# A two-block language model on one core: the second block's input projection is woven with its convolution and its sparse attention, padded columns are left out, and 11 of 31 convolution taps go to VectorE

## The reference, cut to what matters

```python
proj = rmsnorm_2(h, mix_norm_g) @ w_in                  # 256 x 1024 @ 1024 x 2328
conv_a, conv_b, q, k_c, v_c, k_s, v_s, k_w, v_w, gate_logits = split(proj)   # 512, 512, 512, 6 x 128, 24
# conformer_conv
u = conv_a * sigmoid(conv_b)
y = causal depthwise convolution of u, 31 taps, 512 channels, + b_dw
y_conv = silu(layernorm(y))
# nsa_mixer: 8 heads of 64, 2 key groups
kc, vc = compress_tokens(k_c), compress_tokens(v_c)     # 15 blocks; a 2048 x 128 product, gelu, 128 x 64
o_cmp = softmax(q kc) vc        # q without rotation
o_slc = softmax(q_r k_s) v_s    # rotated; at 256 tokens every block is selected
o_win = softmax(q_r k_w) v_w    # rotated
y_nsa = g0 * o_cmp + g1 * o_slc + g2 * o_win            # g = sigmoid(gate_logits)
h = h + concat(y_conv, y_nsa) @ w_out
```

## Time and profile before

| | us |
|---|---|
| median of 3 runs | 1765.82 |
| lowest and highest of them | 1763.61 and 4126.84 |
| the profiled execution | 1765.62 |
| its span, first to last instruction | 1763.8 |
| PE busy | 1663.6 (94% of the span) |
| DVE, ACT, POOL busy | 1191.0, 876.0, 288.1 |
| mean granted clock of TensorE, as a share of 2.4 GHz | 0.971 |

### The profile page before, as it was taken

How to read it: one execution, slowest core, us unless ns; L and a number is a source line. 1 busy time by engine, 2 the same in 40 slices (tenths; PEclk the granted TensorE clock), 3 DMA queues, 4 the chain that set the end, 5 groups by cost and what they waited for, 6 DMA issues and landing times.

```text
span 1763.8 us, 32178 instructions
## 1 busy us (share of the span) xinstructions
PE 1663.6 (94%) x10882; PEld 1510.2 (86%) x10882; DVE 1191.0 (68%) x2262; ACT 876.0 (50%) x1596; POOL 288.1 (16%) x205
## 2 busy tenths in 40 slices
PE   8799998999999989899899989999999999999997
PEld 7788886999887878788799989998888899999996
DVE  3777556688755452445557947887999877777776
ACT  4743343666556551445455465554444445445444
POOL 3233220011100013100003864552000000000000
PEclk9889989999999998999999999999999999999999
DMA  7332233555563630005254654445777756555654
GB/s 266 109 99 81 73 93 122 161 169 182 181 196 121 211 96 0 1 27 191 73 179 150 206 166 139 146 136 175 244 239 240 222 187 190 185 186 188 187 183 153
DMA packets 88138, 271.38 MB, mean 154 GB/s; under 512 B 9856, under 2 KB 26624, under 8 KB 87680
## 3 DMA queue, kind: packets, MB, share of 16 engines
q1 hardware_dynamic: 65088, 237.01, 42.3%
q10 hardware_dynamic: 22976, 33.36, 5.8%
HBM read 258.80 MB, written 11.53 MB: 153 GB/s over the span
## 4 chain that ended last, share of the span: by engine, by line
PE 79%; DVE 11%; ACT 5%; issue 3%; DMA 1%; ACTq 1%; POOL 0%; DVEq 0%
PE ps_chunk L468 43%; PE ps_misc L468 19%; PE ps_misc L279 6%; PE ps_chunk L279 6%; PE ps_misc L2095 3%; DVE ffn_arena L1326 1%; ACT w_hi L403 1%; DVE w_lo L410 1%; DVE x_lo L666 1%; PE ps_misc L651 1%; DVE mixers_arena L1900 1%; DVE mixers_arena L1901 1%; DVE mixers_arena L1897 1%; DVE mixers_arena L1896 1%; DVE mixers_arena L1899 0%
## 5 line engine op out<-in xcount | busy, mean ns | idle before, releaser
L403 ACT ACTIVATE w_hi<-raw 128x512 fp32r<-128x512 f32 x900 | 554.4, 630 | 530.1 <-PE ps_chunk L468 329.4
L410 DVE TENSOR_TENSOR w_lo<-raw,w_hi 128x512 fp32r<-128x512 f32 x725 | 518.1, 729 | 312.1 <-ACT w_hi L403 302.7
L468 PE MATMUL ps_chunk<-x_hi,w_hi 128*128 128x256 f32 x1856 | 543.6, 293 | 20.2 <-POOL w_lo L410 10.0
L468 PE MATMUL ps_chunk<-x_hi,w_lo 128*128 128x256 f32 x1856 | 530.9, 286 | 0.0
L468 PE MATMUL ps_chunk<-x_lo,w_hi 128*128 128x256 f32 x1856 | 530.5, 286 | 0.0
L468 PEld LDWEIGHTS ps_chunk<-x_hi,w_hi 128*128 128x128 f32 x1856 | 360.9, 194 | 32.5 <-POOL w_lo L410 15.0
L468 PEld LDWEIGHTS ps_chunk<-x_hi,w_lo 128*128 128x128 f32 x1856 | 361.7, 195 | 2.7 <-issue 0.2
L468 PEld LDWEIGHTS ps_chunk<-x_lo,w_hi 128*128 128x128 f32 x1856 | 361.2, 195 | 0.0
L410 POOL TENSOR_TENSOR w_lo<-raw,w_hi 128x512 fp32r<-128x512 f32 x175 | 228.7, 1323 | 498.5 <-ACT w_hi L403 279.1
L468 PE MATMUL ps_misc<-w_hi,hid_hi 128*128 128x512 f32 x520 | 204.3, 393 | 4.8 <-DVE w_lo L410 4.8
L468 PE MATMUL ps_misc<-w_hi,hid_lo 128*128 128x512 f32 x520 | 203.8, 392 | 0.0
(11 more groups left out here) (338 smaller groups left out, 1792.1 us busy)
## 6 DMA issues: line engine op xcount, KB each, us to landing
raw<-in_stream SPq DMA_DIRECT2D x452, 512.0 KB, 3.6
early_rows<-row ACTq DMA_DIRECT2D x64, 128.0 KB, 2.4
row<-early_rows ACTq DMA_DIRECT2D x64, 128.0 KB, 3.7
memory_kv<-mixers_arena ACTq DMA_DIRECT2D x4, 512.0 KB, 2.9
mixers_arena<-in_cmp_w ACTq DMA_DIRECT2D x1, 2048.0 KB, 7.3
mixers_arena<-memory_kv ACTq DMA_DIRECT2D x4, 512.0 KB, 6.9
mixers_arena<-in_consts ACTq DMA_DIRECT2D x1, 1665.0 KB, 6.9
row<-in_rows ACTq DMA_DIRECT2D x3, 512.0 KB, 5.3
```

What stands on the lines that cost most here:

```text
L403: e.activation(w_hi[q % 2][:, s], raw[q][:, s], ACT.Copy).then_inc(made, 1)
L410: e.tensor_tensor(w_lo[q % 2][:, s], raw[q][:, s], w_hi[q % 2][:, s].bitcast(F32), ALU.subtract).then_inc(made, 1)
L468: last = e.matmul(o, stationary[a], moving[b], start=start and i == 0, stop=stop and i == 2, skip_group_check=True)
```

## The change

1. `MIXERS_2_ORDER`, a string of letters, weaves five generators: d (the five chunks of `w_in_2`, now by `dense`), k (keys, compression, tile 0 of the attention), q (tables, queries, tile 1), c (taps by PE, layer norm) and t (taps by VectorE). `multiply` and the 30 fillers go. Half of the `w_lo` work of these chunks goes from DVE to POOL.
2. The order of the chunks is k_c v_c k_s v_s; k_w v_w gates; q; conv_a; conv_b. Two PSUM pairs are used in turn (`pairs=2`).
3. `widths`: the chunk with the gates is split, multiplied and copied out with 280 columns in place of 512, and the first block's last token chunk with 256.
4. Taps 0 to 19 stay on PE, in diagonals of 10 (POOL, 128 x 1280). Taps 20 to 30 are 4 x 11 instructions of DVE which accumulate in PSUM; the bias and PE's sum are added by DVE as well.
5. The loads of tables and positions are issued ahead of those for compression and have a semaphore of their own.

```diff
+CONV_PE = 20
+MIXERS_2_ORDER = ("ddctkdqdqdkdddddqddddddddkddkdkdkdkkkqdcddddkkdkddkddddkdkddddkddddkddddkddqdqddddddddqdddddddqddqdd"
+                  "ddddddqdddddcqtqccttqttcctqkctqtcqckckctkcktqtqtcttctttqtkqqtkttccckcccccccqcqtckctkcqckccqkqqkckcqc"
+                  "kqckcccqkqcqkccckcqcccckcqkqkccckkqq")
...
+        widths = {STREAM["w_in token"][0] + 2: RK_H * RK_N, STREAM["w_in_2 token"][0] + 1: 280}
...
-            first, _ = multiply("w_in_2 feature", False, t)
-            multiply("w_in_2 token", True)
-            split_chunks(first, 5, act_hooks=(copy_hook(first, chunk_rows(Z2)),))
...
-            keep_warm(30)
-            interleave(conv=(0, 2, conv, 2),
...
+            dense_again(first, STREAM["w_out_2"][0])
+
+            def dense_chunks():
+                yield from dense(*STREAM["w_in_2 token"], True, lambda n: Z2[:, n - first, :], by_k=t, pairs=2)
+                yield from dense(*STREAM["w_in_2 feature"], False, lambda n: Z2[:, n - first, :], pairs=2)
+
+            keys, queries, NS = nsa(Z2, first, causal, seen, seen_add, inv, pos_raw, cmpw1, cmpw2, have_2, have_cmp)
+            conv, taps = conv_module(Z2, first)
+            weave(MIXERS_2_ORDER, dense=(0, 4, dense_chunks()), conv=(2, 2, conv), keys=(4, 2, keys()),
+                  queries=(6, 2, queries()), taps=(0, 2, taps))
...
+            def taps_by_dve():
+                while not made:
+                    yield "early"
+                for j in range(CONV_PE, CONV_K):
+                    for k in range(CONV_T):
+                        tap, src = taps[:, k, j:j + 1], U[:, k, j:j + T]
+                        if j == CONV_PE:
+                            sums = dve.do(lambda e, k=k, tap=tap, src=src: e.tensor_scalar(
+                                sums_at[:, k, :], src, tap, None, ALU.mult), made[0], own=False)
+                        else:
+                            to = Y if j == CONV_K - 1 else sums_at
+                            sums = dve.do(lambda e, k=k, tap=tap, src=src, to=to: e.scalar_tensor_tensor(
+                                out=to[:, k, :], in0=src, scalar=tap, in1=sums_at[:, k, :], op0=ALU.mult,
+                                op1=ALU.add), before[k], own=False)
```

442 lines of the change are left out of this document (249 added, 193 removed).

## The result

The changed kernel takes 1736.93 us (median of four runs, 1736.40 to 1746.03) against 1767.35 for the kernel before on the same chip. The ratio of the two is 0.9847, with a 95% interval of 0.9803 to 0.9891; it compares the means of the runs and leaves out one run of the kernel before that took 4126.84 us, so it is not the quotient of the two medians. The forecast was 1728.6 with a range of 1713 to 1746. The profiled execution took 1736.4 us, span 1734.6.

A forecast was written before the change was run, and what follows sets the result against it. PE's queue was taken to bound the kernel (79% of the chain of waits). The second mixer's stage going from 206.0 to 172.5 (-33.5) and -3.5 in the first block gave -37.0 from 1765.62: 1728.6 us, range 1713 to 1746.

The forecast's parts named there:

- rival A: Second mixer's stage: PE's queue holds, locks don't bite; first-half gaps shrink to 7, middle to 58; 1714 us, chance 0.22.
- First block: Last token chunk of the first projection, 256 columns instead of 512: -3.5 us, bounds 0 and 5.3.
- Taps: Second mixer: 44 fewer taps on PE at 0.43 us each, -19.0 us; DVE's taps at 0.445 each.
- Padding: Second projection's 280-column chunk: 48 matmuls at 0.13 instead of 0.23 us, -4.8 us of PE.
- Start of the stage: PE's gaps at unit 2: 3.5 us for ACT's late split and POOL's half, 1.2 for DVE's half behind the tables.
- Diagonals at the keys: First half: POOL's two diagonals stop two-input DVE instructions; PE waits 5 us at the keys' transposes, bounds 0 and 9.
- Half clock of the front: Projection with early steps: PE at half clock costs 1.7 us after the first gap, 3.4 at the compression.
- Middle: Taps and attention after U: both queues walked in order, 64.5 us plus 1.7 for half clock, 66.2 us.
- End: From the layer norm's first transposes to `w_out_2`: PE's queue unchanged, 25.3 us against 25.5 before.
- Rival B: Second mixer: `w_lo` halves and six diagonals on POOL stop DVE, delaying softmaxes; +15 us, 1744 us, chance 0.22.
- Rival C: Second mixer: the weave starves PE, progress under 0.70 makes the stage slower than before; 1777 us, chance 0.04.
- Rival D: DVE's taps make PE wait, first block's saved columns bring 0; +8, 1737 us, chance within the forecast's and B's.

The follow-up runs named there:

- The run with another order: Changed kernel, second mixer's start reordered: VectorE's first table steps behind unit 2's `w_lo` half, compression loads behind ACT's first `w_hi`; ratio 0.9816.
- the kernel with three edits: Changed kernel with table steps behind unit 2's `w_lo`, compression loads behind ACT's first `w_hi`, first two diagonals behind the last `w_lo`; ratio 0.9778, median 1727.4 us.
- the serial order: Changed kernel without weave: all steps of the second projection first, the other four strands after it in their own order; ratio 1.0001.
- the four edits: The kernel with three edits, plus both halves of `w_lo` by VectorE in the second mixer; ratio to the kernel before 0.9770.

## Why the prediction was right, and where it was not

The range held. I had put 0.55 on faster by over 2% and 0.43 on within 2%, and it is within: the gain was 29 us where I had put 37. Two errors met in the number: the first block gave 2.8 us more than forecast, the stage 10.8 less; that they partly cancel is luck. PE's work in the stage, busy time times clock by the earlier trace rows and the windows above, came to 148.7 us from 176.7, where I had put 146.0. Two sums of the forecast hold slips that change no chance: its dense matmuls add up to 51.1 us and not 51.4, and rival A's own terms to -16 and not -14.

- **First block: mis-sized.** Forecast -3.5 between bounds of 0 and 5.3, measured -5.8 alone. I had priced only PE's matmuls and then deducted for a busy DVE. The fear was groundless: behind the chunk DVE was as busy as before (15.7 of 16.1 us), so none of its work had been hidden beside the wide chunk. The chunk's splits and copy-outs are narrower too (1.08 us became 0.65), which may be the half microsecond beyond PE's 5.3; no run shows it.
- **Taps: right as far as shown.** 19 us for 44 taps. When 40 of them went back, the product of the back grew by 19 us, 17 of them the matmuls by count; the whole kernel lost 26. DVE started a tap every 0.40 us, below my 0.445.
- **Padding: right** in size, 4.8 against 4.
- **Start of the stage: right.** 4.7 forecast, 5.3 measured (2.78 and 2.52), for the reasons given: ACT splits late, POOL writes its half, DVE stands at the tables. The run with another order took 3.4 of it away.
- **Diagonals at the keys: right mechanism.** 5 forecast, 3.6 measured (3.05 and 0.56), and moving them won 2.4. Moving them also showed that I had its price too low: the wait brings half clock with it. In all six kernels whose diagonals stand at the keys a stretch at half clock begins within 1.7 us of the end of that wait, and in the five woven kernels where they stand elsewhere none begins there. The Trainium skill (SBUF — State Buffer, Who interferes with whom) has both sides of this lock: it names copies and `tensor_scalar` among those that can take the shared ports, and our copies, which have one input, stood 3.48 us against 0.88, so that clause is needed and the one on two inputs, which I had used, does not cover them; it says that an instruction with at most one SBUF input outside those modes does not contend, and the taps kept 0.40.
- **Half clock of the front: the term that failed.** I put 5.1 us (1.7 after the first wait, 3.4 at the compression). It was six stretches of 3.4 us, 10.2: one after the first waits, one at 591.7 around the wait for the keys, four from 601.9 through the compression and 5.5 us beyond. Before, the compression had the same matmuls and 10.2 us at half clock. I counted two thirds of that and nothing for what the wait ahead adds. This is 5.1 of the 10.8.
- **Middle: nearly right.** 66.2 forecast with 1.7 of half clock, 69.6 measured with 3.4. So 1.7 is clock and 1.7 is in the turns, which is what my walk is worth. The first big scores came at 22 instead of 20.6, for the reason named.
- **End:** 26.2 against 25.3. 0.81 of it is a wait for ACT's copies at 727.8.

In sum the half clock is 6.8 us of the 10.8 and all other terms 4.0. **Rival A** is where the kernel with three edits arrived in the front (72.0), but its middle of 58 was never near: PE has 58.8 of work there and waits 7.4 more, 6.8 of it for ACT's copies. **Rival B** (DVE and POOL take over, 1744) had its mechanism seen and its price refuted: twice the diagonals cost PE 1.9 us of waits, and the clock 2.3. **Rival C** did not come; 148.7 us of work in 183.3 is 0.81, over its 0.70. **Rival D** came out in the number, 1737, and not in the cause: DVE's taps did bring their 19 us.

What I had not weighed at all is what the weave protects. I took it as hiding waits; the serial order shows that it is worth some 20 us of waits and 11 of clock. By my own terms I would have forecast the serial kernel 9 us slower, and it was 27.

What stays open: which event ahead decides where a stretch of half clock falls, and how long it lasts (6.8 to 13.7 us, from within one and the same compression, in the woven kernels). Runs of one kernel differ in their mean clock by up to 0.011. So a difference of 5 us or less between two of these kernels is not a ranking, the one between the three edits and the four among them.

## What to carry to other kernels

Look for half clock over a run of small matmuls in the trace of before, price it as found there, and then ask what stands around it: here a weave with wide matmuls was worth 11 us more than the 20 of waits that it hid, and a wait of PE ahead of such a run cost more than its own length. When an instruction of VectorE with two SBUF inputs, or a copy, stands beside GpSimd, look who waits for it: 5 us of GpSimd cost PE 3.6 at the keys, and 16 us more of it cost 1.9 beside the softmaxes. Compare kernels part by part, by length times granted clock and by PE's idle time, before you believe a ratio of a few tenths of a per cent, and look at the parts that you did not touch as well; and when work is taken off an engine, narrow the other engines' share of it too in the sum.

## What the runs showed of the hardware that I had not expected

- Half clock with PE busy without a gap: 13.70 of 13.70 us at 0.50, 8.2 of them over the compression's 30-column matmuls. The same matmuls in portions between 512-column ones ran at 1.00 (14.00 of 14.00 us busy).
- The time of one and the same kernel goes with its mean clock: 1725.3 us at 0.974 and 1742.4 at 0.965, 1734.1 at 0.974 and 1750.1 at 0.963, and with the four edits 1717.6 at 0.976 and 1729.2 at 0.971. 0.001 of clock is 1.5 to 2.3 us between these pairs.
- GpSimd is held up as well: a diagonal beside the taps took 2.34 us, and this one of the changed kernel, which began 0.02 us behind a product of DVE with two inputs (L752, 1.22 us), took 3.40:

```profile
708.99 3.40 POOL L1596 TENSOR_TENSOR mixers_arena<-ident_iota,col 128x1280 f32<-128x1280 f32 x1 [8.23 <-PE ps_chunk L284]
```

- A GpSimd instruction that waits for nothing goes as early as its queue lets it: freed of its halves of `w_lo`, it ran 27 us earlier and stopped DVE at a place where PE did wait.
